# Aligned tensors, split products for the latent projections, and one key tile in the second block

## The reference

```python
q = (_rms_norm(q_lat, q_norm) @ w_uq).reshape(B, S, H, MLA_NOPE + MLA_ROPE)      # 384 -> 8 heads of 64 + 32
kv = (_rms_norm(kv_lat, kv_norm) @ w_ukv).reshape(B, S, H, MLA_NOPE + MLA_V)     # 256 -> 8 heads of 64 + 64
q_nope, q_pe = q[..., :MLA_NOPE], q[..., MLA_NOPE:]
k_nope, v = kv[..., :MLA_NOPE], kv[..., MLA_NOPE:]
q_pe, k_pe = rope(q_pe), rope(k_pe)                   # k_pe: one for all heads
o = causal_attention(concat(q_nope, q_pe), concat(k_nope, k_pe), v)
```

## Time and profile before

| | us |
|---|---|
| timed runs | 3354.37, 3358.22, 3360.66 |
| median | 3358.22 |
| span of the profiled execution | 3355.3 |
| TensorE busy in it | 3210.7 (96%) |
| ScalarE, VectorE, GpSimd busy | 1184.3, 1508.7, 1484.2 |

### The profile page before, as it was taken

One profiled execution on the slowest core, in us unless ns is written; L12 is line 12 of the kernel. 1 busy time (PEld: TensorE's weight loads), 2 busy tenths in 40 slices (PEclk: granted clock), 3 DMA queues, 4 the chain that ended last, 5 costly groups with the idle time before them and its releaser, 6 DMA issues. The chain is left out here.

```text
span 3355.3 us, 51795 instructions
## 1 busy us (share of the span) xinstructions
PE 3210.7 (96%) x21120; PEld 2517.9 (75%) x21120; DVE 1508.7 (45%) x2374; ACT 1184.3 (35%) x1940; POOL 1484.2 (44%) x820
## 2 busy tenths in 40 slices
PE   8899999999999999999998989999999998899999
PEld 6784786888678747868876756788888875678787
DVE  7633384999575333949996235300100022520000
ACT  6324433422353434252225445322122243532221
POOL 4431553454353325445442276344234434745454
PEclk9999999999999999999999999999999999999999
DMA  3011122555210112235543100111121111023222
GB/s 129 9 34 57 57 101 76 210 200 192 74 63 4 46 63 70 94 108 194 207 151 110 65 26 27 56 64 59 55 70 63 63 61 50 15 81 101 92 97 94
DMA packets 77611, 284.18 MB, mean 85 GB/s; under 512 B 8736, under 2 KB 8736, under 8 KB 76864
## 3 DMA queue, kind: packets, MB, share of 16 engines
q1 hardware_dynamic: 77376, 280.88, 24.5%
HBM read 278.75 MB, written 2.10 MB: 84 GB/s over the span
## 5 line engine op out<-in xcount | busy, mean ns | idle before, releaser
L131 POOL TENSOR_TENSOR lows<-ring,highs 128x1024 fp32r<-128x1024 f32 x376 | 939.5, 2500 | 1552.0 <-ACT highs L123 1517.5
L155 PE MATMUL ps<-x_high,highs 128*128 128x512 f32 x2080 | 832.6, 400 | 32.4 <-ACT highs L123 13.6
L158 PE MATMUL ps<-x_low,highs 128*128 128x512 f32 x2080 | 816.0, 392 | 0.0
L123 ACT ACTIVATE highs<-ring 128x1024 fp32r<-128x1024 f32 x376 | 397.0, 1056 | 725.9 <-PE ps L155 382.7
L155 PEld LDWEIGHTS ps<-x_high,highs 128*128 128x128 f32 x2080 | 393.4, 189 | 131.6 <-issue 35.6
L158 PEld LDWEIGHTS ps<-x_low,highs 128*128 128x128 f32 x2080 | 393.4, 189 | 85.4 <-issue 4.8
L1788 DVE CUSTOM_DVE_ANT_0 BR<-BR 128x1024 f32<-128x1024 f32 x144 | 288.6, 2004 | 6.8
L2828 DVE TENSOR_TENSOR hidden_scratch<-ps,hidden_scratch 128x512 f32<-128x512 f32 x44 | 30.5, 692 | 546.5 <-PE ps L2138 538.3
L722 PE MATMUL ps<-x_high,lows 128*128 128x512 f32 x1024 | 252.9, 389 | 0.0
L722 PEld LDWEIGHTS ps<-x_high,lows 128*128 128x128 f32 x1024 | 192.2, 188 | 39.9
L2704 DVE SCALAR_TENSOR_TENSOR BR<-ps,mod,BR 128x512 f32<-128x512 f32 x72 | 47.4, 662 | 368.7 <-PE ps L167 368.7
(11 more groups left out here) (443 smaller groups left out, 5580.0 us busy)
## 6 DMA issues: line engine op xcount, KB each, us to landing
ring<-in_w SPq DMA_DIRECT2D x414, 512.0 KB, 3.5
BR<-in_ada SPq DMA_DIRECT2D x72, 512.0 KB, 3.5
merging<-in_ada SPq DMA_DIRECT2D x24, 512.0 KB, 3.4
X<-in_xT SPq DMA_DIRECT2D x4, 512.0 KB, 6.5
X<-in_memT SPq DMA_DIRECT2D x2, 1024.0 KB, 5.5
BR<-in_cond SPq DMA_DIRECT2D x4, 512.0 KB, 4.6
out<-BR SPq DMA_DIRECT2D x8, 256.0 KB, 4.4
cst<-in_cst SPq DMA_DIRECT2D x1, 1408.0 KB, 7.7
```

Source lines behind the costliest of these rows:

```text
L123: nc.scalar.activation(self.high(n), self.chunk(n), ACT.Copy).then_inc(self.hi_made, 1)
L131: nc.gpsimd.tensor_tensor(self.low(n), self.chunk(n), self.high(n).bitcast(F32), ALU.subtract).then_inc(self.lo_made, 1)
L155: mm = nc.tensor.matmul(ps, high, xhigh, start=start, stop=False)
L158: nc.tensor.matmul(ps, high, xlow, start=False, stop=False)
```

## The change

1. **Places.** Constants and parameters are padded to multiples of 16 columns (`LINE`), as are the small tensors; 32 bytes are put ahead of `merged_*`. All large tensors then begin at multiples of 64 bytes. `X` is cut into two tensors, of which the upper one is given up during the latent stage for the split latents.
2. **Latent stage.** All 11 chunks are split. Queries come as six full tiles, the rotary parts of four heads each in the first two, the 64-row parts of two heads each in the other four; keys as four tiles of two heads. The latents are normalised and then split too (ScalarE's `latent_high`, VectorE's `latent_low`). Two `swap` matmuls of 128x128 take the place of eight of 32x32. The attention's opening asks for one split chunk instead of two.
3. **Second block.** One key tile holds both key heads (10 chunks instead of 11). The doubled copies are written by VectorE at the end: four adds of 64x512 for the rotated key, four multiplies of 64x256 for the context key. The order in the stage moves up by one tile.

The core of the diff (bookkeeping left out):

```diff
-NCST = _at
+NCST = -(-_at // LINE) * LINE
...
-SPLIT1 = [FIRST[_name] + _i for _name, _n in (("rwkv", RW_TILES), ("mla", 6), ("beside", 12), ("gates", 16)) for _i in range(_n)]
+SPLIT1 = [FIRST[_name] + _i for _name, _n in (("rwkv", RW_TILES), ("mla", 11), ("beside", 12), ("gates", 16)) for _i in range(_n)]
...
             if beside is not None:
-                beside.stream.hi(nc, act, beside.first + PARTS)
+                beside.stream.hi(nc, act, beside.first + 1)
...
+                def two_tiles(n, banks, first, ks, done):
+                    stream.wait_high(pe, n)
+                    for i, bank in enumerate(banks):
+                        for j in range(ks):
+                            pe.wait_ge(S("q_low"), first + j + 1)
+                            with_high(nc, PS[:, bank, :], tile_of(stream.high(n), ks * i + j), QNH[:, first + j, :], QNL[:, first + j, :], j == 0,
+                                      used if i == 0 and j == 0 else None)
+                    stream.wait_split(pe, n)
+                    for i, bank in enumerate(banks):
+                        for j in range(ks):
+                            mm = nc.tensor.matmul(PS[:, bank, :], tile_of(stream.low(n), ks * i + j), QNH[:, first + j, :], start=False, stop=(j == ks - 1))
+                        mm.then_inc(done, 1)
...
+                two_tiles(nq, (2, 3), 0, 3, S("q"))
                 pe.wait_ge(S("kpe"), 1)
...
+                two_tiles(nq + 1, (0, 4), 0, 3, S("q"))
+                turn_queries(0)
+                turn_queries(1)
+                two_tiles(nq + 2, (2, 3), 0, 3, S("q"))
...
             def _(act):
-                    stream.hi(nc, act, n0 + min(t + 3, 6))
+                    stream.hi(nc, act, n0 + t + 3)
...
                 deviation(0, 384)
+                for t in range(3):
+                    latent_high(t)
...
                 deviation(1, 256)
+                for t in range(3, 5):
+                    latent_high(t)
+                stream.hi(nc, act, nq + 2)
+                for i in range(2):
+                    act.wait_ge(S("q"), i + 1)
+                    a.activation(QP[:, i, :], PS[:, 2 + i, :], ACT.Copy).then_inc(S("q_pe"), 1)
...
             def _(pool):
-                stream.lo(nc, pool, n0 + 6)
+                stream.lo(nc, pool, nk + 1)
                 pool.wait_ge(S("kp_rot"), 1)
...
+        kept.enter_context(nc.sbuf_tensor(f"merged_line{layer}", [P, LINE // 2], F32, side="right"))
...
-        tiles = [("q", i) for i in range(4)] + [("k", i) for i in range(2)] + [("v", 0)] + [("p", i) for i in range(2)] + [("f", i) for i in range(2)]
+        tiles = [("q", i) for i in range(4)] + [("k", 0), ("v", 0)] + [("p", i) for i in range(2)] + [("f", i) for i in range(2)]
...
-                    v.tensor_tensor(dst, XT(27 + i % 2), XT(29 + i % 2), ALU.add).then_inc(S("rotated"), 1)
+                    if i < 4:
+                        v.tensor_tensor(dst, XT(27 + i % 2), XT(29 + i % 2), ALU.add).then_inc(S("rotated"), 1)
+                    else:
+                        for g, rows in enumerate(HALVES):
+                            for copy in HALVES:
+                                v.tensor_tensor(dst[copy, g, :], XT(27 + i % 2)[rows], XT(29 + i % 2)[rows], ALU.add).then_inc(S("key_rotated"), 1)
```

More of the change, by code:

```diff
@@ L464, in _ @@
             if beside is not None:
-                beside.stream.lo(nc, pool, beside.first + PARTS)
+                beside.stream.lo(nc, pool, beside.first + 1)
             for i in range(N if beside is None else N + 2):
@@ L1341, in _ @@
                 latent_sum(1, 3, 2)
-                pe.wait_ge(S("kpe"), 1)
[L1343 to L1354, removed]
-                            mm.then_inc(used, 1)
-                    mm.then_inc(S("q"), 1)
@@ L1357, in _ @@
[L1357 to L1364, removed]
-                                     start=True, stop=True).then_inc(S("q_swapped"), 1)
-                    if h >= 2:
-                        pe.wait_ge(S("k_out"), h - 1)
-                    for k in range(2):
-                        mm = nc.tensor.matmul(PS[0:64, 4 + h % 2, :], stream.chunk(n)[:, h * 128 + k * 64:h * 128 + (k + 1) * 64],
-                                              QN[:, 3 + k, :], start=(k == 0), stop=(k == 1))
-                        if h == 0 and k == 0:
-                            mm.then_inc(used, 1)
-                    mm.then_inc(S("k"), 1)
@@ L1385, in _ @@
+                stream.wait_split(pe, nv)
+                for q in range(4):
+                    for j in range(2):
+                        mm = nc.tensor.matmul(PS[:, 4 + q, :], QNH[:, 3 + j, q * P:(q + 1) * P], stream.low(nv)[:, j * 512:(j + 1) * 512], start=False, stop=(j == 1))
                     mm.then_inc(S("v"), 1)
@@ L2939, in consts1 @@
     put("causal", np.where(col > row, -1e30, 0.0).astype(np.float32))
-    for a in range(32):
-        out[64 + (a + 16) % 32, CCOL["swap"] + a] = 1.0
+    put("swap", (row == (col ^ 16)).astype(np.float32))
     inv = (np.float32(10000.0) ** (-np.arange(0, 32, 2, dtype=np.float32) / np.float32(32))).astype(np.float32)
-    out[64:96, CCOL["freq"]] = np.concatenate([inv, inv])
-    out[64:80, CCOL["sign"]] = -1.0
-    out[80:96, CCOL["sign"]] = 1.0
+    out[:, CCOL["freq"]] = np.tile(inv, 8)
+    out[:, CCOL["sign"]] = np.where(i // 16 % 2, 1.0, -1.0)
     for k, e in enumerate((64e-5, 1e-6, 1e-5, 0.0)):
@@ L2991, in chunks2 @@
     table = dft(T)
-    out[11:11] = [table[:, a:a + CW] for a in range(0, table.shape[1], CW)]
+    out[IN_TILES:IN_TILES] = [table[:, a:a + CW] for a in range(0, table.shape[1], CW)]
     return np.stack(out if l else out[:EARLY] + out)
```

272 lines of the change are left out of this document (166 added, 106 removed).

## The result

The changed kernel takes 3307.66 us (median of four runs, 3301.06 to 3310.06) against 3357.05 for the kernel before beside it: ratio 0.9848, 95% interval 0.9834 to 0.9862. That is 49 us less, where I had forecast 72: inside the stated range (3267 to 3309), outside the forecast's own (3272 to 3301). In the profiled executions the span falls from 3355.3 to 3304.5 us, 50.8 less.

The account below looks back on a forecast made before the run. TensorE, busy 3210.7 of 3355.3 us, was taken to bound the kernel; 35 (latent stage) + 21 (second block) + 16 (places) = 72 us off gave a span of 3283, median 3286, range 3267 to 3309.

Parts of the forecast that it names:

- Latent stage: Latent stage of each layer: TensorE's shorter list less new waits saves 17.3 us per layer, 35 us for two.
- both waits: Latent stage: TensorE waits 1.1 us for the first query chunk's low part, 5.0 us for the second's high part.
- the half clock: Latent stage, behind the new 5.0 us gap: TensorE's clock at half level, counted as 1.7 us.
- the tightest: Latent stage, value chunk: its low part, behind GpSimd's eight key copies (5.5 us), is still made in time.
- Second block: Second block's input: one key tile fewer, with its square sums and a swap, saves 10.5 us per layer, 21 us.
- its cover: Second block: the last tile, 8.3 us (5.5 in the second layer), still hides VectorE's 3.4 us of rotation.
- an attention that never regains its lead: Rival, attention's weight stream: stays one chunk behind, each tile waits for its split, 83 us, giving 3369; chance 0.03.
- The places: Matmuls on tensors moved to multiples of 64 bytes: shorter distance saves 16 us, between 0 and 20.
- 2592 in all: Count of 512-column matmuls on hidden, branches, merged and mixed parts; at 6.2 ns each 16 us.
- For the other engines [...] I count nothing: The places: other engines' instructions on moved tensors, beside TensorE, were counted at nothing.
- the places do nothing: Rival: distances come from what runs beside the tensors, not where they lie; 3302 us, chance 0.14.
- Splits waited for one by one: Rival, latent stage: each of five new chunks makes TensorE wait 3.45 us, 11 more per layer; 3308, chance 0.13.

Follow-up runs that it names:

- first profile: Profile of the changed kernel against the kernel before: span 3304.5 us against 3355.3; its timed median 3307.66 us, ratio 0.9848.
- in the second: The changed kernel run and profiled once more, unedited: 3304.68 us, ratio 0.9848 to the kernel before.
- experiment 3: Changed kernel with its moved tensors 32 bytes further, again 32 bytes past a multiple of 64: 3303.12 us, 0.9841 of the kernel before.
- experiment 7: Changed kernel with 14 low parts per merging stage moved from GpSimd to VectorE and the moved tensors 32 bytes further: 3300.53 us, ratio 0.9823.
- 8: Changed kernel with 64 bytes put in front of the moved tensors, all still at multiples of 64: 3295.35 us, 0.9818 of the kernel before.

## Why the prediction was right in direction and too large

- *Latent stage*, forecast 17.3 us per layer: 15.2 and 15.6 in the first profile, whose stages began at the same clock as before. The mechanism was right: both waits came where forecast, at 1.01 and 5.04 us. The term was 2 us too large per layer: the half clock cost 2.4 us (12 matmuls in 5.14 us, at 0.227 they are 2.7) instead of 1.7; and the value chunk, which I called the tightest and gave no wait, waited 0.72, since GpSimd's eight copies took 7.5 us, not 5.5. What is left, some 0.6 us, is spread over the later matmuls:

```profile
293.45 7.53 POOL L1529 COPY BR<-X 32x512 f32<-32x512 f32 x8
301.06 2.38 POOL L127 TENSOR_TENSOR lows<-ring,highs 128x1024 fp32r<-128x1024 f32 x1
```

- *Second block*, forecast 10.5 per layer: 10.8 in both layers of the first profile, 10.8 and 9.6 in the second. Right, with its cover. The rival of an attention that never regains its lead fell: the attention stages are within 2.5 us of before.
- *The places*, forecast 16: nothing net. This is the step that failed. The rows were rightly read (0.234 to 0.2277 on `hidden_parts`, and back when moved); the failure is in "2592 in all", where I multiplied the distance by all matmuls as if TensorE set the pace wherever they stand, and in "For the other engines [...] I count nothing". In the merging stages, with 768 of them, VectorE was 97% and 95% busy, and the new pace made its meetings with GpSimd worse; there the 5 us that I had counted came out as some 6 lost (experiment 3). I had read VectorE's share over the whole span and left the stage unread, although its rows were in the trace. The term was too large besides: with VectorE out of the way the places are worth 7 to 11 us (experiment 7), since on the branches and the merged parts the distance changed by some 3 to 5 ns instead of 6.2, and since the 256-column matmuls, which I had left out, took back a part. The rival "the places do nothing" named the right size for a wrong reason.
- *Not in the sum*: the first feed-forward stage got 3.6 us shorter even with the places moved back; there the distance on the context's parts is 118 ns instead of 120, which for 1056 matmuls makes 2 of it, and it went back to 120 when 64 bytes were added. Against that, in the first profile the first layer's output was 3.0 us longer (2.0 of it is the wait shown above), the second block's first attention 2.5 (granted clock 0.94 instead of 0.99), the second layer's attention 1.7 and the start 1.3.
- *The range was met by luck*: the time came to lie in it because it was drawn around two rivals, and the runs refute the mechanism of both. "Splits waited for one by one" had 3308, the measured time; but TensorE waited 5.0, 1.0 and 0.7 us per layer in the latent stage, and not 3.45 for each of five chunks. "The places do nothing" had 3302; the distances do follow the places.

Together: 30.8 + 21.6 is 52.4, and all other stages came out 1.6 us longer between the two profiles, which makes their 50.8; by the timed medians it is 49 (first set of runs) and 53 (second). What stays open is which place of a tensor gives which distance: neither 64 nor 128 bytes explains all that experiments 3 and 8 show.

## What to carry to other kernels

Before a saving on the busiest engine is counted, read every engine's busy time in that very stage: an engine at 45% of the span was at 97% in the stage that mattered, and the saving came back as waiting. An instruction's duration is not a constant: look for the longest and shortest of its group, and for what runs beside the long ones; here moving a third of GpSimd's work in the stage onto the fuller engine made that engine less busy. A faster producer shifts when things meet, so a stage in which two engines hold each other up can get longer by an edit that removes work.

## What was not expected of the hardware

- VectorE instructions with two SBUF inputs that begin while GpSimd's low part runs end only after it, 119 of 120 in the changed kernel: 1.22 becomes up to 3.4 us (1024 columns), 0.69 up to 2.9 (512 columns); begun ahead of it, they keep their time, and the low part takes longer. The multiply of a PSUM operand by an SBUF one in the same stage kept 0.69 throughout.
- The distance of float32r matmuls follows where the moving tensor begins: 512 columns on `hidden_parts` 227.7 ns at a multiple of 128 bytes, 229.1 at 64 past one, 233.3 at 32 (234.1 in the kernel before); 256 columns 119.5, 113.8 and 116.8 (118.0). The place does not tell all: `branches_high` has 229.4 at 64 past a multiple of 128, but 235.3 at a multiple.
